# A fused two-block layer on one core: one 256-column accumulator per output tile, weight slabs split two ahead, and the modulation rows moved from VectorE to GpSimd

## What is computed

```python
# block 1
mod = silu(c) @ w_ada + b_ada; shift, scale, gate = split(mod, 3)
h = rmsnorm(x, pre_g) * (1 + scale) + shift
q, k, v, gate_a, u, gate_p = split(h @ w_in)
y_a = windowed_gqa(q, k, v) * silu(gate_a);  y_p = pool(u) * silu(gate_p)
g_a, g_p = split(sigmoid(h @ w_merge + b_merge))
x = x + gate * rmsnorm((g_a * (y_a @ w_br_attn) + g_p * (y_p @ w_br_pool)) @ w_out, post_g)
# block 2
mod = silu(c2) @ w_mod + b_mod; sh1, sc1, g1, sh2, sc2, g2 = split(mod, 6)
h = rmsnorm(x) * (1 + sc1) + sh1
... = split(h @ w_in2)          # attention (q, k, v), linear attention (q, k, v, decay), gates
x = x + g1 * rmsnorm((sig(g_a) * (o_a @ w_br_a) + sig(g_b) * (o_b @ w_br_b)) @ w_out2)
h = rmsnorm(x) * (1 + sc2) + sh2
x = x + g2 * rmsnorm(conv_ffn(h))   # h @ w_up, causal width-3 conv, silu(gate) * val, @ w_down
```

## Time and profile before

| | us |
|---|---|
| median of 3 runs (2519.30 to 2521.08) | 2520.79 |
| the profiled execution | 2521.72 |
| span of its trace, first to last instruction | 2519.9 |
| PE busy | 2312.4 (92%) |
| VectorE busy | 1789.0 (71%) |
| ScalarE busy | 1153.7 (46%) |
| GpSimd busy | 94.1 (4%) |

### The profile page before, as it was taken

How to read it: one execution, slowest core, us unless ns; L and a number is a source line. 1 busy time by engine, 2 the same in 40 slices (tenths; PEclk the granted TensorE clock), 3 DMA queues, 4 the chain that set the end, 5 groups by cost and what they waited for, 6 DMA issues and landing times.

```text
span 2519.9 us, 32064 instructions
## 1 busy us (share of the span) xinstructions
PE 2312.4 (92%) x12836; PEld 1982.0 (79%) x12836; DVE 1789.0 (71%) x2282; ACT 1153.7 (46%) x1637; POOL 94.1 (4%) x113
## 2 busy tenths in 40 slices
PE   2499999999995889999999999997999999989997
PEld 1388888888784768888888888886888888878886
DVE  6767777779854787777677888646777777764444
ACT  1343455555445345454455455445444444434443
POOL 1000000000000000000011100000000000000000
PEclk8599999999996989999999999998999999999998
DMA  9867778878843757578777788743555555556662
GB/s 380 353 229 271 260 260 286 292 269 308 307 158 120 258 175 259 202 248 293 263 262 256 253 291 306 268 167 117 186 198 184 171 197 184 189 158 188 188 184 80
DMA packets 313032, 580.67 MB, mean 230 GB/s; under 512 B 12187, under 2 KB 105167, under 8 KB 308533
## 3 DMA queue, kind: packets, MB, share of 16 engines
q1 hardware_dynamic: 300224, 535.86, 62.3%
q0 software_dynamic: 11328, 40.26, 4.9%
q10 hardware_dynamic: 1332, 2.51, 0.3%
HBM read 557.61 MB, written 20.97 MB: 230 GB/s over the span
## 4 chain that ended last, share of the span: by engine, by line
PE 60%; DVE 9%; ACT 4%; issue 2%; DMA 0%; DVEq 0%; ACTq 0%
PE gemm L1607 38%; PE gemm L1608 19%; DVE w_lo L985 2%; DVE mod_acc L978 1%; PE extra L1430 1%; ACT w_hi L676 1%; ACT quad_work L676 1%; PE extra L1422 1%; DVE proj L1057 1%; ACT scores L676 0%; ACT operand_main L676 0%; DVE small L1198 0%; DVE scores L1195 0%; DVE proj L1054 0%; PE extra L1516 0%
## 5 line engine op out<-in xcount | busy, mean ns | idle before, releaser
L1607 PE MATMUL gemm<-operand_main,w_hi 128*128 128x512 f32 x4880 | 1740.0, 404 | 72.9 <-issue 26.5
L1608 PE MATMUL gemm<-operand_main,w_lo 128*128 128x256 f32 x4880 | 1329.3, 283 | 0.0
L1607 PEld LDWEIGHTS gemm<-operand_main,w_hi 128*128 128x128 f32 x4880 | 911.9, 191 | 281.0 <-issue 44.3
L985 DVE TENSOR_TENSOR w_lo<-w_stage,w_hi 128x1024 fp32r<-128x1024 f32 (+2 forms) x774 | 876.0, 1160 | 361.1 <-ACT w_hi L676 360.6
L676 ACT ACTIVATE w_hi<-w_stage 128x1024 fp32r<-128x1024 f32 (+2 forms) x776 | 766.3, 1007 | 653.5 <-PE gemm L1608 652.4
L1608 PEld LDWEIGHTS gemm<-operand_main,w_lo 128*128 128x128 f32 x4880 | 934.7, 192 | 30.1
L978 DVE SCALAR_TENSOR_TENSOR mod_acc<-mod_stage,c_silu,mod_acc 128x1024 f32<-128x1024 f32 x224 | 285.4, 1315 | 0.6 <-DMA mod_stage<-in_w_mod 0.6
L676 ACT ACTIVATE low_part<-gemm 128x256 f32<-128x256 f32 x329 | 125.4, 384 | 326.7 <-PE gemm L1607 302.6
L1607 PE MATMUL gemm<-ffn_hidden,w_hi 128*128 128x512 f32 x704 | 249.8, 401 | 9.8 <-issue 9.8
L1608 PE MATMUL gemm<-ffn_hidden,w_lo 128*128 128x256 f32 x704 | 196.1, 282 | 0.0
L1607 PEld LDWEIGHTS gemm<-ffn_hidden,w_hi 128*128 128x128 f32 x704 | 132.5, 190 | 41.7 <-issue 10.1
(11 more groups left out here) (198 smaller groups left out, 1214.5 us busy)
## 6 DMA issues: line engine op xcount, KB each, us to landing
w_stage<-in_w_in SPq DMA_DIRECT2D x128, 1024.0 KB, 6.2
mod_stage<-in_w_mod SPq DMA_DIRECT2D x192, 512.0 KB, 5.6
w_stage<-in_w_up SPq DMA_DIRECT2D x88, 1024.0 KB, 5.0
w_stage<-in_w_down SPq DMA_DIRECT2D x64, 704.0 KB, 4.8
w_stage<-in_w_ada SPq DMA_DIRECT2D x32, 1024.0 KB, 8.0
w_stage<-in_w_merge SPq DMA_DIRECT2D x32, 1024.0 KB, 5.5
w_stage<-in_w_out SPq DMA_DIRECT2D x32, 1024.0 KB, 5.5
mod_stage<-in_w_ada SPq DMA_DIRECT2D x32, 512.0 KB, 6.0
```

What stands on the lines that cost most here:

```text
L985: tt(WL[:, s1 % 2, c0:c1], WST[:, s1 % 4, c0:c1], WH[:, s1 % 2, c0:c1].bitcast(F32), ALU.subtract)\
L1607: hi = lambda **kw: mm(bank[:, :], WH[:, s % 2, c0:c0 + P], X_[:, k, :], **kw)
L1608: lo = lambda **kw: mm(bank[:, T:2 * T], WL[:, s % 2, c0:c0 + P], X_[:, k, 0:T], **kw)
```

## The change

The change rewrites how a product is laid out and who does what around it.

- **Matmuls.** The 512-column matmul becomes two of 256 columns with the same `w_hi`, and all three products of a weight tile (hi x hi, hi x lo, lo x hi) are summed in one accumulator of 256 columns. Two output tiles share a bank; two groups of banks alternate. The number of matmuls and of weight loads of a product goes from two to three for each weight tile.
- **Results.** ScalarE copies two tiles at a time out of the accumulator straight to their place (`evac`); VectorE does so only where it multiplies (the branches) or convolves (the up projection). `low_part` and the adds are gone.
- **Buffers and lead.** Five stage buffers, `w_lo` written over its own stage buffer, three of `w_hi`. The splits run two slabs ahead instead of one. The load of a slab now waits for `slab_used` of the slab five before, that is for TensorE.
- **Modulation rows.** For parts 2 to 8, VectorE's one operation on a half row becomes two on GpSimd: a TENSOR_SCALAR that multiplies the half row in place, and a TENSOR_TENSOR that adds it to `mod_acc`. Parts 0 and 1 stay on VectorE.
- **The rest.** The down projection uses slabs of four tiles in eleven steps and waits for `ffn_hidden` quad by quad; the last hidden quad is made during its first slabs. The taps of the convolution read the accumulator. Some copies on ScalarE (`take_wait`, the key and value of a head) are gone.

```diff
-    def __init__(self, w, col, step, slabs, operand, evac, tiles=QUAD, chunks=QUAD, bank0=0, **kw):
+RAW, HIS, AHEAD = 5, 3, 2
+        self.banks = (tiles + 1) // 2
+        self.by = "dve" if evac in ("merge_a", "merge_b", "ffn") else "act"
...
-                    sp.wait_ge(lo_made, n * 2 - 6)
+                    sp.wait_ge(slab_used, 2 * (t - MOD0_ROWS - RAW) + 2)
...
-            def mod_row(sg, i, r):
-                    stt(acc, MST[:, half, :], CSI[:, bass.ds(i * rows + c, 1)], acc, ALU.mult, ALU.add).then_inc(mod_rows, 1)
+            def mod_row(ph, r):
+                for half in range(2):
+                    pool.wait_ge(m_landed[half], 16 * (ph.mod0 // 2 + r + 1))
+                    positive(pool, mod_rows, n2 - 1)
+                    nc.gpsimd.tensor_scalar(MST[:, half, :], MST[:, half, :], CSI[:, c:c + 1], None, ALU.mult).then_inc(mod_scaled, 1)
+                    pool.wait_ge(mod_scaled, n2 + 1)
+                    nc.gpsimd.tensor_tensor(acc, acc, MST[:, half, :], ALU.add).then_inc(mod_rows, 1)
...
+                cut = 4 if ph.name == "gates2" else len(ph.slabs)
+                    mod_rows_of(ph, 0, cut)
+                    store_gate(1, ph.groups[0])
+                    mod_rows_of(ph, cut, len(ph.slabs))
+                    pool.wait_ge(gs["sq"], i + 1)
+                    nc.gpsimd.tensor_tensor(VF[:, 0:2, :], VF[:, 0:2, :], VF[:, 2:4, :], ALU.add).then_inc(gs["sq2"], 1)
...
-                                        hi = lambda **kw: mm(bank[:, :], WH[:, s % 2, c0:c0 + P], X_[:, k, :], **kw)
-                                        lo = lambda **kw: mm(bank[:, T:2 * T], WL[:, s % 2, c0:c0 + P], X_[:, k, 0:T], **kw)
+                            mm(acc, hi, x_[:, k, 0:T], start=(k == 0 and m % 2 == 0), stop=False, skip_group_check=True)
+                            mm(acc, hi, x_[:, k, T:2 * T], start=False, stop=False, skip_group_check=True)
+                            ins = mm(acc, lo, x_[:, k, 0:T], start=False, stop=(k == nk - 1), skip_group_check=True)
...
+            for n in range(AHEAD):
+                split_lo(n)
...
+                    if ph.slab0 + s + AHEAD < len(slabs):
+                        split_lo(ph.slab0 + s + AHEAD)
```

964 lines of the change are left out of this document (436 added, 528 removed).

## The result

The changed kernel took **2796.49 us** in the median, the kernel before, run beside it, 2521.08: a ratio of 1.108 (95% interval 1.106 to 1.110), 275 us more. The forecast was 2630 us and its range ended at 2730. The direction was right; the size was too small by a factor of 2.5. The first profile of the changed kernel was taken at a granted clock of 0.625 and can't be laid beside the one of before, so the profile read here is of a second execution of the same kernel (2789.74 us, span 2787.3).

What follows compares the result with a forecast made beforehand. TensorE was taken as the bound, busy nearly throughout. Body excesses and `gates2` gave +124 us, less 9.8 and 5.7: +108.5 on 2521.72, so 2630 us, 4.3% slower; eight-in-ten range 2535 to 2730 us.

Steps and rivals of the forecast that it cites:

- The price of TENSOR_SCALAR: Modulation rows on GpSimd: multiplying a half row takes 1.4 us, with the 2.26 us addition 3.66 us a half row.
- GpSimd alone would not be late: Bodies with rows: four half rows take 14.6 us on GpSimd, below the 22.6 us of the products.
- The rule of the sum: Bodies with rows: GpSimd's half rows and VectorE's two-input operations exclude each other, so their summed time must fit the body.
- The stretches: Excess by body: +24 for 15 bodies, `in` +19, `merge` +8, `branch1` +8, `qkvb` +11, `branch2` +18 us, `out2` 0.
- The order in `gates2`: `gates2`: GpSimd takes slab 6's row before the `gla_v` addition; TensorE stands 10.6 us; +7, +2 for `gla` steps, four times: +36.
- The matmuls: All products: two 256-column matmuls for one of 512 cost 0; the other end, 0.120 us each, was +35 us.
- the 9.79 us ahead of `down`: Entrance of `down`: the wait for the last `ffn_hidden` quad, needed now only in the eleventh slab, goes: -9.8 us.
- the 11.62 behind `gla_gate`: Behind `gla_gate`: with the second slab split before VectorE's chain, 5.7 us of products run under it: -5.7 us.
- The 44.9 of the forecast: `up`: a sign that the forecast is right, the stretch still taking 44.9 us a body.
- A gain put at nothing: VectorE loses 224 half-row operations of about 1.2 us, which it had time for, so nothing is gained.
- The multiplication is as dear as the addition: Rival, rows on GpSimd: 4.52 us a half row, 27.7 against 22.6 us in a body, 2790 us; chance 0.10.
- The faster case: Rival: the lead hides everything, half rows below some 3.2 us and `gla5` not held, 2495 us; chance 0.09.

Runs made afterwards that it cites:

- Six fills: Changed kernel with each half row's two GpSimd operations replaced by six zero fills that read nothing: 2688.47 us, 1.0665 of the kernel before.
- experiment 1: Changed kernel with the modulation rows back on VectorE, one fused operation for each half row, none on GpSimd: 2542.57 us, 1.0073 of the kernel before.
- three fills: Changed kernel with each half row's two GpSimd operations replaced by three zero fills of the sum: 2569.18 us, 1.0179 of the kernel before.
- 7: Changed kernel with the modulation rows on VectorE and at most four, not five, first-norm rows in flight: 2524.52 us, 1.0014 of the kernel before.

## Why the prediction was wrong

- **The price of TENSOR_SCALAR: the step that failed.** I took 1.4 us between a MEMSET at 0.9 and an addition at 2.26, because a multiplication by a column reads one tensor where the addition reads two. It takes 2.85 us undisturbed, outside both bounds. The number of inputs doesn't order GpSimd's operations. A half row is 5.2 us alone instead of 3.66, and 6.2 beside VectorE's work, so that four of them are 24.8 us in a body whose products take 23.0 (64 steps of 0.360). (The addition alone was nearly right: 2.26 worked out, 2.34 measured.) A right price alone would not have mended the sum, though: the forecast's sum has 2630 us for a half row of 3.66 and 2790 for one of 4.52; on the same line 5.1 gives some 2900, an estimate, and 100 too much.
- **"GpSimd alone would not be late" was asked of the average only.** Undisturbed, four half rows (20.8 us) would still fit. Six fills of 5.74 us, which read nothing, just fit as well (23.0), and yet they cost 146 us: with no slack left, every place where TensorE needs something from GpSimd is late. Of these I had only `gla_v`. The end of a norm's rows, where TensorE needs the sum at once, was no term (46.0 us of waits), nor was GpSimd's own small load of `positions` behind the rows (11.3 us, and 11.7 for the chain behind it, 23 of the 25 that `qkv2` loses).
- **The rule of the sum (GpSimd's and VectorE's operations exclude each other) was half right.** It is true of the additions: 3.43 instead of 1.19 in the earlier trace rows, 6.13 behind two of them here. For the multiplication it is too strong: it keeps `w_lo` back for its first microsecond only (`w_lo` 1.32 in the mean, +12 us over fills), and is itself lengthened by a `w_lo` under way (3.62 against 2.95 us). The Trainium skill (SBUF — State Buffer, "Who interferes with whom") puts every GpSimd instruction that reads SBUF under the rule and calls it an exclusive lock. The additions agree. For TENSOR_SCALAR the contention is there too, but not for the whole instruction, and there the measurement decides. Where the sum fits the body, the products lose nothing even with the additions; the chains that TensorE waits for lose.
- **The stretches.** For the rows on GpSimd (changed less experiment 1), forecast and measured: first products +25, 23; `merge` +8, 20; `branch1` +8, 16; `out1` +6, 23; `qkv2` +5, 25; `qkvb` +11, 21; `og` +6, 15; `branch2` +18, 14; `out2` 0, 6; `gates2` +36, 89. Two are near, but the first products not for the reason given: there TensorE loses by GpSimd's rate, at the sum (17.4 us), not in the bodies. (`branch1` is 7 by its own numbers, 24.2 + 1.4 against 23.8.)
- **The order in `gates2`** was the best term in kind: named rows, engine and waiting matmul as they came. It was given 10.6 us of standing for each body and had 13 (51.8 / 4), and undoing it gave 50 us against a forecast of 28 (four times 7; the other 8 of the 36 were the `gla` steps). The remaining 40 are the `gla` steps behind VectorE (20.3 us of waits in four bodies, +2 us for each body in the forecast, so 8) and the rows themselves.
- **The matmuls: I took the wrong end.** The earlier trace rows had 0.12 for a 256-column matmul with its own load; I took three times 0.118 and 0. It is 0.120, and alone +36, the upper end that I had given as +35. The range had room for it.
- **What was right:** `up` has no wait, the 9.79 us ahead of `down` are gone from the changed kernel, and of the 11.62 behind `gla_gate` 4.7 are left with the rows on VectorE, 6.9 gone where 5.7 were forecast. `up` runs at 46.2 us a body. The 44.9 of the forecast came from a window that leaves out the segment's first ten microseconds; by the matmul records it was 45.5 before (1724.7 to 2228, less 2.95 of wait, by eleven), and the 0.7 more are the third matmul (128 steps, 0.006 each).
- **What no term held:** the start, +18.5, of which 12 to 15 are the fifth row in flight. The diff showed the ring's size; I priced it in the products alone.
- **A gain put at nothing:** VectorE was said to have had time for its half rows. In `qkvb` it had not: with the rows gone from VectorE and little on GpSimd (three fills, or the multiplication alone) that stretch is 10 to 20 us shorter than in experiments 1 and 7, and TensorE's waits for `scores` in the whole execution are 2.8 us with the three fills against 16.4 in experiment 1.
- **The rivals.** "The multiplication is as dear as the addition" gave 2790, within 7 us of the result, and had 0.10. Its direction was right and its mechanism in part: it takes 2.26 for the multiplication (2.85 measured) and charges it with shutting VectorE out for its whole length, which it does for its first microsecond. Two errors of opposite sign met. The faster case is refuted: it wanted a half row below 3.2 us.

The range failed because the one unknown price had been bounded by rows of other operations, and its ends were then used as if they were measured. An operation that the trace doesn't show deserved an upper end beyond its most similar neighbour.
